# A two-block decoder layer on one core: first loads in another order, ring units moved, and products of constants put in TensorE's gaps

## The reference

```python
mod = jax.nn.silu(c) @ ada_w + ada_b
...
sh_m, sc_m, g_m, sh_f, sc_f, g_f = jnp.split((mod + ada_table[layer])[:, None, :], N_MOD, axis=-1)
h = _rms(x, norm_mix_pre[layer]) * (1 + sc_m) + sh_m
y, v_first = _rwkv7_mix(h, ...)
x = x + g_m * _rms(y, norm_mix_post[layer])
h = _rms(x, norm_ffn_pre[layer]) * (1 + sc_f) + sh_f
f = _conv_ffn(h, ...)
x = x + g_f * _rms(f, norm_ffn_post[layer])
```

## Time and profile before

| | |
|---|---|
| runs shown | 2059.53, 2066.36, 2067.49 us |
| median | 2066.36 us |
| the profiled execution | 2064.75 us, its span 2063.1 us |
| TensorE busy | 1958.8 us, 95% |
| VectorE busy | 1389.0 us, 67% |
| ScalarE busy | 897.1 us, 43% |
| mean granted TensorE clock | 0.975 of 2.4 GHz |

### The profile page before, as it was taken

How to read it: one execution, slowest core, us unless ns; L and a number is a source line. 1 busy time by engine, 2 the same in 40 slices (tenths; PEclk the granted TensorE clock), 3 DMA queues, 4 the chain that set the end, 5 groups by cost and what they waited for, 6 DMA issues and landing times.

```text
span 2063.1 us, 34272 instructions
## 1 busy us (share of the span) xinstructions
PE 1958.8 (95%) x13392; PEld 1703.7 (83%) x13392; DVE 1389.0 (67%) x1981; ACT 897.1 (43%) x1457; POOL 121.3 (6%) x119
## 2 busy tenths in 40 slices
PE   3999999898898988999999999999989999999999
PEld 2888888787786866888888888888878888888887
DVE  5986459643765987777777776444466567767876
ACT  2335321022233545555555555444454435535553
POOL 2000001100002310000000000000010000001200
PEclk8999999999999988999999999999999999999999
DMA  9986224565743954545555556555536444445553
GB/s 403 400 352 215 102 86 160 223 258 232 288 166 125 425 205 163 183 183 183 187 184 193 186 186 221 191 184 194 191 106 241 164 163 177 150 152 216 184 184 123
DMA packets 59078, 419.34 MB, mean 203 GB/s; under 512 B 6560, under 2 KB 6688, under 8 KB 12448
## 3 DMA queue, kind: packets, MB, share of 16 engines
q1 hardware_dynamic: 54656, 384.34, 50.3%
q0 software_dynamic: 3888, 27.26, 3.3%
q10 hardware_dynamic: 432, 6.29, 0.7%
HBM read 411.58 MB, written 6.29 MB: 203 GB/s over the span
## 4 chain that ended last, share of the span: by engine, by line
PE 91%; DVE 4%; DMA 2%; issue 1%; ACT 1%; SPq 0%; POOL 0%; DVEq 0%; ACTq 0%
PE ps L700 41%; PE ps L701 21%; PE ps L677 12%; PE ps L781 4%; PE ps L775 1%; PE ps L761 1%; DMA ring<-in_wv 1%; PE ps L752 1%; DMA bk<-in_ada 1%; PE ps L1007 1%; PE ps L1066 1%; PE ps L797 1%; DVE ring L1665 1%; PE ps L934 1%; PE ps L664 0%
## 5 line engine op out<-in xcount | busy, mean ns | idle before, releaser
L700 PE MATMUL ps<-x_pair,whi 128*128 128x512 f32 x2464 | 881.8, 402 | 14.4 <-DVE x_pair L1721 9.9
L701 PE MATMUL ps<-x_pair,wlo 128*128 128x256 f32 x2464 | 693.8, 282 | 0.0
L1687 DVE TENSOR_TENSOR wlo<-ring,whi 128x1024 fp32r<-128x1024 f32 x468 | 547.6, 1206 | 102.9 <-ACT whi L1227 96.5
L700 PEld LDWEIGHTS ps<-x_pair,whi 128*128 128x128 f32 x2464 | 465.2, 189 | 135.0 <-issue 21.9
L1227 ACT ACTIVATE whi<-ring 128x1024 fp32r<-128x1024 f32 x468 | 462.4, 1031 | 96.4 <-PE ps L701 93.8
L701 PEld LDWEIGHTS ps<-x_pair,wlo 128*128 128x128 f32 x2464 | 467.9, 190 | 0.3
L1234 ACT ACTIVATE px<-ps 128x256 f32<-128x256 f32 x202 | 77.8, 385 | 475.0 <-PE ps L701 475.0
L700 PE MATMUL ps<-hid_pair,whi 128*128 128x512 f32 x688 | 238.8, 394 | 0.0
L701 PE MATMUL ps<-hid_pair,wlo 128*128 128x256 f32 x688 | 190.6, 277 | 0.0
L677 PE MATMUL ps<-mixb,ring 128*128 128x256 f32 x640 | 146.6, 391 | 13.6 <-DMA ring<-in_wv 12.0
L700 PEld LDWEIGHTS ps<-hid_pair,whi 128*128 128x128 f32 x688 | 129.0, 188 | 30.2 <-DVE wlo L1687 0.3
(11 more groups left out here) (291 smaller groups left out, 2286.3 us busy)
## 6 DMA issues: line engine op xcount, KB each, us to landing
ring<-in_fi SPq DMA_DIRECT2D x86, 1024.0 KB, 4.8
ring<-in_zin SPq DMA_DIRECT2D x52, 1024.0 KB, 4.8
ring<-in_ada SPq DMA_DIRECT2D x42, 1024.0 KB, 6.9
ring<-in_fo SPq DMA_DIRECT2D x32, 1024.0 KB, 4.8
bk<-in_ada SPq DMA_DIRECT2D x22, 1024.0 KB, 10.3
ring<-in_wr SPq DMA_DIRECT2D x16, 1024.0 KB, 4.8
ring<-in_wv SPq DMA_DIRECT2D x16, 1024.0 KB, 4.9
ring<-in_wo SPq DMA_DIRECT2D x16, 1024.0 KB, 8.9
```

The source lines that it names most:

```text
L700: mm(ps[:, bank, 0:2 * S], w_h, pair_k, start=first and k == 0, stop=False)
L701: m = mm(ps[:, bank, 0:S], w_l, pair_k[:, 0, :], start=False, stop=last and k == n - 1)
L1687: V.tensor_tensor(wlo[:, hf % WB, 0:m], ring[:, u % RING, 1024 * x:1024 * x + m], whi[:, hf % WB, 0:m].bitcast(F32), ALU.subtract).then_in ...
```

## The change

It has six parts. (1) `const` is loaded in two pieces, the columns from `cos` on after all rows; `w1`, `a1` and `g1` are no loads of their own but lie behind the `k` columns in each row of `wkr` (1984 columns instead of 1536). (2) ScalarE squares `x` before the SiLU of `c`; VectorE takes the reciprocal of `rms(0)` before its first products, and `mixes(i-1)` between the two products of `dots(i)`. (3) `ar` is laid out so that 256 tokens of a tile are contiguous, and two sums by head are made for 128 tokens at a time. (4) `RV` holds six `v` units before its first `ada` unit, then two after each; 22 in place of 24 fall in the v stage, and the scan's chunks take 4, 6, 6, 4 in place of 5, 5, 4, 4. (5) `gated_y(q)` comes in round `q` and no longer in round `q+1`. (6) `keep_clock` multiplies constants 10, 18 and 8 times, into a PSUM bank that nobody reads. The waits follow these.

```diff
 for _k in range(NT):
-    RV += [("v", _k)] + [("ada", len(RV) - NT - _k + _j) for _j in range(0 if _k < 2 else 1 if _k < 8 else 3 if _k < 10 else 2)]
-SCAN_DOTS = (5, 5, 4, 4)
-RV += [("ada", 24 + _k) for _k in range(sum(SCAN_DOTS))]
+    RV += [("v", _k)] + [("ada", len(RV) - NT - _k + _j) for _j in range(0 if _k < 5 else 2)]
+RING_DOTS = len(RV) - 2 * NT
+SCAN_DOTS = (4, 6, 6, 4)
+RV += [("ada", RING_DOTS + _k) for _k in range(sum(SCAN_DOTS))]
...
-            sp.dma_start(cst[:], t["const"]).then_inc(ld_par, 16)
+            sp.dma_start(cst[:, 0:EARLY], t["const"][:, 0:EARLY]).then_inc(ld_cst, 16)
...
-                sp.dma_start(ring[:, i % RING, 0:KO * P], t["wkr"][i]).then_inc(ld_row[i % RING], 16)
+                sp.dma_start(ring[:, i % RING, 0:ROW], t["wkr"][i]).then_inc(ld_row[i % RING], 16)
...
-            sp.dma_start(lora_w1, t["w1"]).then_inc(ld_lora, 16)
-            sp.dma_start(lora_a1, t["a1"]).then_inc(ld_lora, 16)
-            for k in range(2):
-                sp.dma_start(flat_c[:, 2048 * k:2048 * (k + 1)], t["g1"][k]).then_inc(ld_lora, 16)
...
+            def keep_clock(n, bank):
+
+                for _ in range(n):
+                    mm(ps[:, bank, 0:S], ident, const("smask"), start=True, stop=True)
...
+            def all_sums_by_head(src, bank):
+
+                for tt in range(TT):
+                    for i in range(NT):
+                        m = mm(ps[:, bank, tt * NH + 2 * i:tt * NH + 2 * i + 2], src(i)[:, tt * P:(tt + 1) * P], const("blk2"),
+                               start=True, stop=True)
+                return m
...
-            pe.wait_ge(ld_par, 32)
+            pe.wait_ge(ld_cst, 16)
             rms(0, mixb)
...
             rms(1, None, NT)
+            keep_clock(10, 6)
             rms(2, mixb)
+            keep_clock(18, 6)
...
             for k in range(5):
                 p_pair(k)
+            keep_clock(8, (TILE["zk"] + 3) % BANKS)
...
+            act.wait_ge(ld_x, 16)
+            squares(0, mixa)
             act.wait_ge(ld_c, 16)
             A(cb[:], cb[:], ACT.Silu).then_inc(silu_c, 1)
-            act.wait_ge(ld_par, 32)
-            act.wait_ge(ld_x, 16)
-            squares(0, mixa)
...
                     dot_into(m, ada_slot(0, s))
+                    if j == 0 and i:
+                        mixes(i - 1)
...
+            rec(0)
             dve.wait_ge(silu_c, 1)
-            dots(0)
-            rec(0)
-            for i in range(1, NT):
+            for i in range(NT):
                 dots(i)
-                mixes(i - 1)
             mixes(NT - 1)
...
-                if q:
-                    gated_y(q - 1)
-                if q in (4, 6):
-                    y_lo_part((q - 4) // 2)
+                gated_y(q)
+                if q in (2, 4, 6):
+                    y_lo_part(q // 2 - 1)
                 if q == 5:
                     lo_part("wo", 0)
-            gated_y(7)
-            y_lo_part(2)
             y_lo_part(3)
```

More of the change, by code:

```diff
@@ L461, in _ @@
                 row(i)
+            sp.dma_start(cst[:, EARLY:], t["const"][:, EARLY:]).then_inc(ld_late, 16)
             def load(u, src, width):
@@ L762, in sums_by_head @@
                 return m
-            pe.wait_ge(ld_par, 32)
+            def all_sums_by_head(src, bank):
[5 more added lines that the diff above has]
+            pe.wait_ge(ld_cst, 16)
             rms(0, mixb)
-            pe.wait_ge(ld_lora, 64)
-            hidden = [("w", lora_w1, LORA), ("a", lora_a1, LORA), ("g", flat_c[:, 0:2048], P), ("g", flat_c[:, 2048:4096], P)]
+            hidden = [("w", KO * P, LORA), ("a", KO * P + LORA, LORA), ("g", ROW - 2 * P, P), ("g", ROW - P, P)]
             for i in range(NT):
                 pe.wait_ge(mix_b, 4 * (i + 1))
-                for n, (name, w, m) in enumerate(hidden):
-                    last = mm(ps[0:m, n // 2, (n % 2) * S:(n % 2 + 1) * S], w[:, i * m:(i + 1) * m], mix_slot(name, i),
+                pe.wait_ge(ld_row[i % RING], 16 * (i // RING + 1))
+                for n, (name, o, m) in enumerate(hidden):
+                    last = mm(ps[0:m, n // 2, (n % 2) * S:(n % 2 + 1) * S], ring[:, i % RING, o:o + m], mix_slot(name, i),
                               start=i == 0 and n % 2 == 0, stop=i == NT - 1, skip_group_check=True)
@@ L800, in _ @@
             pe.wait_ge(k_sq, NT)
-            for c in range(NCH):
-                m = sums_by_head(c, lambda i: ar[:, i, c, 1, :], 4)
-            m.then_inc(hs_sum, 1)
+            all_sums_by_head(lambda i: ar_i[:, i, 1, :], 4).then_inc(hs_sum, 1)
             pe.wait_ge(mix_b, 5 * NT)
@@ L893, in _ @@
                     pe.wait_ge(bonp, 1)
-                    for c in range(NCH):
-                        m = sums_by_head(c, lambda i: rkr[:, i, c * CH:(c + 1) * CH], 4)
-                    m.then_inc(bon_sum, 1)
+                    all_sums_by_head(lambda i: rkr[:, i, :], 4).then_inc(bon_sum, 1)
                 elif k == 8:
@@ L1881, in _ @@
             dve.sem_inc(bonp, 1)
-            for j in range(24):
+            for j in range(RING_DOTS):
                 ada_ring(j)
@@ L1893, in _ @@
                 for j in range(SCAN_DOTS[c]):
-                    ada_ring(24 + sum(SCAN_DOTS[:c]) + j)
+                    ada_ring(RING_DOTS + sum(SCAN_DOTS[:c]) + j)
                 dve.wait_ge(c_u, c + 1)
@@ L2192, in _ @@
             gate(NT - 1)
-_LAID = ["c", "const", "param", "x", "ada", "wkr", "w1", "w2", "a1", "a2", "g1", "wk", "wr", "wv", "g2", "wo", "fi", "fo",
+_LAID = ["c", "const", "param", "x", "ada", "wkr", "w2", "a2", "wk", "wr", "wv", "g2", "wo", "fi", "fo",
          "zin", "wp", "p", "zo", "pg"]
@@ L2240, in lay_out @@
     out["ada"] = np.ascontiguousarray(f["ada_w"].T).reshape(96, P, D)
-    out["w1"], out["a1"] = rows(f["rwkv_w1"][0]), rows(f["rwkv_a1"][0])
     out["w2"], out["a2"] = f["rwkv_w2"][0], f["rwkv_a2"][0]
-    out["g1"], out["g2"] = units(f["rwkv_g1"][0]), halves(f["rwkv_g2"][0])
+    out["g2"] = halves(f["rwkv_g2"][0])
     out["wr"], out["wk"], out["wv"] = (units(f["rwkv_w_rkv"][0, n]) for n in range(3))
-    out["wkr"] = np.ascontiguousarray(f["rwkv_w_rkv"][0, 1][:, :KO * P]).reshape(NT, P, KO * P)
+    out["wkr"] = np.concatenate([f["rwkv_w_rkv"][0, 1][:, :KO * P], f["rwkv_w1"][0], f["rwkv_a1"][0], f["rwkv_g1"][0]],
+                                axis=1).reshape(NT, P, ROW)
     out["wk"] = out["wk"][KO:]
```

38 lines of the change are left out of this document (25 added, 13 removed).

## The result

The changed kernel takes 2049.84 us (median of 20 runs, 2036.63 to 2063.32), the kernel before 2065.99 (20 runs, 2055.53 to 2073.26). The ratio is 0.9929, with a 95% interval of 0.9909 to 0.9949: 16 us faster by the medians and 15 by the ratio, where 24 were forecast. A second series gave 2045.75 against 2063.6, 0.9912 [0.9885, 0.9939]. The profiled execution took 2056.57 us, 8.2 less than that of before.

The account below looks back on a forecast made before the run. TensorE, busy 95% of 2063.1 us, was taken as the bound, leaving its waits, slow-clock stretches and unneeded work. Seven terms summed to 24.1 us off 2064.75, giving 2040.6 us, range 2031 to 2050.

Parts of the forecast that it names:

- term 1: First stage: earlier loads and reciprocal let the first step start at 37.1 us, not 43.75; 6.6 us gained.
- term 2: Sums by head, two places: 64 matmuls with weights of 128 columns replace 128; 1.0 us gained.
- term 3: v stage: the wait before v projections, its low clock and two small gaps go; 10.6 us gained.
- The rule by the weights' columns: Sums by head: weight load time goes with columns, so half as many wider loads save nothing; sum 1.0 us less.
- Terms 4 and 5: Scan: earlier VectorE copy, net 1.1 us gained; gate and start of wo: 3.9 earlier less 2.8, 1.1 us gained.
- The gap of 4.2 us in wo and its low clock: First wo tile: TensorE stands still 4.2 us after its first half and the clock falls; 2.8 us lost.
- Term 6: First residual: products of constants cover the gaps around rms(2) and before fi; 0.9 us gained.
- Term 7: Second residual: eight products of constants in the 4.52 us wait before zk keep the clock up; 2.8 us gained.
- B: Rival: clock stays up in wo's gap and around sums by head; 2.8 and up to 5 us more, 2033; chance 0.11.
- D: Rival: in the first stage's steps, row loads starve TensorE; slower than before, 2081 us; chance 0.02.

Follow-up runs that it names:

- f_dots: Changed kernel with the first two ada products on VectorE moved ahead of the first norm's reciprocal, no early table load; 2043.4 us, one run.
- u_order: Changed kernel with the old order of the ring's v and ada units and the old scan product numbers (5, 5, 4, 4); 2057.7 us.
- f_gap2: Changed kernel with nine products of constants, run once, between the two halves of the first wo tile; 2045.0 us.
- u_clock: Changed kernel without the three groups of products of constants (all keep_clock lines gone); 2049.2 us.
- f_mix: Changed kernel with the sums by head taken apart and set among projection products of r and v tiles; 2041.6 us.

## Why the prediction was wrong

The sign and most of the places were right; the sum was 8 us too large by the medians and 9.4 by the ratio. The median of 2049.84 us lies at the upper end of the range of 2031 to 2050; taken by the ratio, on the 2066.36 us of the kernel before, it is 2051.7 and outside. The stages, means of the two profiles of each kernel, against the terms:

| term | forecast | measured |
|---|---|---|
| 1, first stage (end of the steps) | 6.6 | 156.2 - 153.3 = 2.9 |
| 2 and 3, sums and v stage | 1.0 + 10.6 | 361.3 - 356.0 = 5.3 |
| 4, scan; 5, gate before wo's second half | 1.1 + 3.9 | 148.6 - 143.8 = 4.8 |
| 5, low clock in wo; 6, first residual | -2.8 + 0.9 | 116.6 - 118.8 = -2.2 |
| 7, second residual (fo's end to the end) | 2.8 | 551.3 - 549.9 = 1.4 |

Together 12.2 us. The medians say 16 and 18; two profiles of each kernel can't give the sum closer than that, since the paces and the length of the `v` stage differ between executions. The steps that failed are the costs of the first stage (term 1), the price of the new sums (term 2) and the last `v` tiles, taken as unchanged (term 3); together 10.0 of the 11.9 us that are missing.

- **Term 1 failed,** in the step "The reciprocal ended at 28.35 and now ends at 22.1": that took ScalarE to be free for the root. The SiLU now stood between squares and root, and the Sqrt table was loaded behind the wait for TensorE's sum, on the path, 1.28 us. And in the step that costed the mixes at 4.2 us "as more of them now lie beside GpSimd": from the first mix to the first step it took 5.7, and GpSimd 16.5 in place of 14.1. I had the order right (all three products in or behind GpSimd's stretch), but did not ask what that order throws away: 7.8 us of an idle VectorE. `f_dots` shows it. The 2.9 us measured are below the bound of 5.
- **Term 2 failed** in the step that set 64 of them at 0.125 us, "8.0 us for 64", against the 9.3 us of the old form, "1.3 us less at each of two places". The 9.3 us of the old form hold its stretch at the low clock, the 0.125 us hold none. At the full clock 128 at 58 ns are 7.4 us and 64 at 112 ns are 7.2, so there was next to nothing to gain. The rule by the weights' columns, with its 1.0 less, came nearer: nothing was gained, and a block even costs some 0.6 more at the same fall of the clock. The bonus sums, moreover, went from 8.8 us to 10.7, since the clock fell 3.3 us into the block and not 4.7; the tile behind was 1.6 us shorter for it, so that from `v` tile 6 to 8 it takes 25.9 and 25.8 us as before.
- **Term 3** was right where it looked and wrong in what it took as unchanged. Up to the start of `v` tile 6 8.2 us were gained (no wait there), and 2.1 from tile 8 to 13 (the two small gaps), together 10.3 for the 10.6 forecast. But from tile 13 to the end it took 30.2 and 32.1 us, where it had taken 26.1 and 26.3. The step that failed is "its 2.97 us stay", which left these tiles otherwise as they were. TensorE stood 2.8 to 3.1 us under "issue" (idle time for which the profile shows no wait) in tile 13, 1.6 in the kernel before, and behind this and the wait of 2.9 the clock was low: the last tile ran in 8.6 and 10.1 us, where it took 7.17. The ring's order is not the cause of the longer idle time, as `u_order`, with the old order, has 3.0 us of it and takes 29.4 us from tile 13 on. Why the idle time is longer in the changed code stays open. The ten profiles with the new order take 27.0 to 32.1 there.
- **Terms 4 and 5** came out in sum, by luck. The scan gave 0.1 and not 1.1: TensorE's waits for VectorE's copy fell from 3.2 us to 1.5 and 0.6 in the two profiles, but the stage from 104.8 only to 105.2 and 104.1. In the first of them idle time under "issue" rose from 5.6 us to 7.7, in the second it did not; where the rest went stays open, the more so as `u_order` has the scan 4 to 5 us longer with the old numbers of products. The gate gave 4.7 and not 3.9, as rounds take 3.8 us, bound by TensorE and not by the 3.0 estimated for VectorE and GpSimd.
- **The gap of 4.2 us in wo and its low clock** were near the forecast: 3.7 us, and 1.5 and 2.8 us lost in the two profiles (by `wo` at the same pace), for 2.8. `f_gap2` shows the cause.
- **Term 6** gave nothing, for 0.9 forecast. `fi` still began 2.15 us behind the last product, and the granted clock was 0.52 in the window from 774 to 776. The pairs at the low clock cost 1.8 us there, 2.5 and 2.2 before, but from `wo`'s last product to `fo`'s first it takes 518.7 and 518.9 us at the long pace, and took 519.3 and 518.2.
- **Term 7:** `zk` starts 0.3 us later than it could without the products (1.6 in the first profile), and the block of `pp` ahead of them took 10.5 and 11.3 us in place of 8.8, at a clock that now fell there. That it does so without the products too (`u_clock`, 10.5) shows that they are not its cause; what is stays open. What the products themselves gave is 0.5 us by the changed kernel's two profiles against `u_clock`, 1.2 by the other eleven.

Of the rivals, B named the largest thing left in the kernel, the sums by head that pull the clock down, at "up to 5"; `f_mix` found 10.6 by `v` tile 8. D, rows starving TensorE, did not come up in any profile, even with a first step at 31.5.

## What to carry to other kernels

Before pricing an earlier operand, list what each engine does in the gap that it leaves: work that is there already, in the wrong order, is worth more than the transfer. A block of narrow products counts as busy and still loses the clock; spread it among wide ones. And before a difference is explained, compare stages, and learn from several profiles of unaltered code how far each stage differs by itself; two profiles were too few here for the `v` stage.
